# Corner copies ahead of the gates, modulation blocks ahead of turned vectors and decay, in a two-layer mixer and expert kernel

## The reference

```python
mod = jax.nn.silu(c) @ ada_w + ada_b
sh1, sc1, g1, sh2, sc2, g2 = jnp.split(mod[:, None, :], 6, axis=-1)
h = (_rms(x, norm1_g) * (1.0 + sc1) + sh1).astype(dtype)
z = h @ w_in                       # 16 column groups of 512, and a few gate columns
...                                # z is cut into p['m_q'], ..., p['n_vw'], p['n_g']
y_m = mlstm_mixer(...)             # conv on q and k, gates i and f, decay matrix, sigmoid(o)
y_b = moba_mixer(...)
y_r = retention_mixer(...)
y_n = nsa_mixer(...)               # compressed, selected (slc) and window (win) branches
y = jnp.concatenate([y_m, y_b, y_r, y_n], axis=-1).astype(dtype) @ w_out
x = x + g1 * y
h2 = (_rms(x, norm2_g) * (1.0 + sc2) + sh2).astype(dtype)
return x + g2 * hier_moe(h2, ...)  # 32 experts, every token to two of one group
```

## Time and profile before

| | us |
|---|---|
| median of 3 runs | 1665.14 |
| lowest, highest | 1665.05, 1674.46 |
| the profiled execution | 1668.25 |
| its span, first to last instruction | 1666.1 |
| TensorE busy | 1393.0 (84%) |
| VectorE busy | 595.8 (36%) |
| ScalarE busy | 187.7 (11%) |

### The profile page before, as it was taken

One profiled execution on the slowest core, in us unless ns is written; L12 is line 12 of the kernel. 1 busy time (PEld: TensorE's weight loads), 2 busy tenths in 40 slices (PEclk: granted clock), 3 DMA queues, 4 the chain that ended last, 5 costly groups with the idle time before them and its releaser, 6 DMA issues.

```text
span 1666.1 us, 17839 instructions
## 1 busy us (share of the span) xinstructions
PE 1393.0 (84%) x7389; PEld 760.7 (46%) x7389; DVE 595.8 (36%) x927; ACT 187.7 (11%) x459; POOL 31.4 (2%) x35
## 2 busy tenths in 40 slices
PE   5998999979999999998876776777677667767767
PEld 4666888758556854473422322223223223223223
DVE  4556684676445457422211221121120121122113
ACT  2001221102012100121100100100100101001001
POOL 0000000000000000010000000000000000000000
PEclk9999999989999999999988887787788788787788
DMA  9996686667758677869999999999999999999997
GB/s 397 427 426 259 251 342 272 257 246 280 268 220 328 234 291 299 361 253 421 424 429 428 428 429 428 429 429 428 428 428 428 428 429 428 428 429 429 428 429 293
DMA packets 44536, 611.90 MB, mean 367 GB/s; under 512 B 4896, under 2 KB 5168, under 8 KB 6736
## 3 DMA queue, kind: packets, MB, share of 16 engines
q1 hardware_dynamic: 42848, 604.00, 87.5%
q0 software_dynamic: 1072, 6.44, 0.9%
q10 hardware_dynamic: 576, 0.89, 0.1%
HBM read 609.21 MB, written 2.10 MB: 367 GB/s over the span
## 4 chain that ended last, share of the span: by engine, by line
PE 49%; DMA 45%; DVE 5%; issue 1%; ACT 0%; SPq 0%; POOL 0%; DVEq 0%
DMA ring<-in_exp_w 31%; DMA Zpad<-in_exp_w 10%; PE W L671 8%; PE W L658 7%; PE W L650 7%; PE M L1092 5%; PE W L1000 5%; DMA ring<-in_stream 3%; PE W L624 2%; PE A L1110 2%; PE W L1044 2%; DVE tail L1441 2%; PE W L976 2%; PE M L634 2%; PE W L1057 2%; PE M L1064 1%
## 5 line engine op out<-in xcount | busy, mean ns | idle before, releaser
L1441 DVE SCALAR_TENSOR_TENSOR tail<-ring,small,tail 128x512 f32<-128x512 f32 x300 | 225.6, 752 | 10.5
L1092 PE MATMUL M<-ring,g1b 128*32 128x512 f32 x1024 | 148.3, 711 | 62.9 <-DMA ring<-in_exp_w 62.9
L1374 DVE TENSOR_TENSOR consts<-A,tail 32x512 f32<-32x512 f32 x128 | 87.9, 686 | 162.5 <-PE A L1110 159.5
L658 PE MATMUL W<-ring,buf_h 128*128 128x512 f32 x320 | 140.7, 598 | 0.0
L1952 DVE SCALAR_TENSOR_TENSOR tail<-tail,M 128x128 f32<-128x128 f32 x32 | 9.2, 288 | 295.6 <-ACT tail L1351 295.6
L1110 PE MATMUL A<-Zpad,tail 128*32 128x512 f32 x512 | 84.5, 793 | 36.3 <-DMA Zpad<-in_exp_w 31.9
L650 PE MATMUL W<-buf_h,ring 128*128 128x256 f32 x512 | 112.0, 379 | 0.2 <-DMA ring<-in_stream 0.2
L1064 PEld LDWEIGHTS M<-consts,tail 128*128 128x128 f32 x512 | 68.4, 208 | 92.1 <-ACT tail L1353 60.0
L650 PEld LDWEIGHTS W<-buf_h,ring 128*128 128x128 f32 x512 | 96.7, 190 | 13.3 <-issue 0.4
L1092 PEld LDWEIGHTS M<-ring,g1b 128*32 128x32 f32 x1024 | 30.8, 119 | 146.5 <-DMA ring<-in_exp_w 90.4
L1092 PE MATMUL M<-Zpad,g1b 128*32 128x512 f32 x512 | 74.9, 713 | 27.0 <-DMA Zpad<-in_exp_w 27.0
(11 more groups left out here) (311 smaller groups left out, 1301.0 us busy)
## 6 DMA issues: line engine op xcount, KB each, us to landing
ring<-in_stream SPq DMA_DIRECT2D x88, 2048.0 KB, 10.3
ring<-in_exp_w SPq DMA_DIRECT2D x88, 2048.0 KB, 38.3
Zpad<-in_exp_w SPq DMA_DIRECT2D x64, 2048.0 KB, 32.1
PPY<-in_exp_w SPq DMA_DIRECT2D x24, 2048.0 KB, 30.8
tail<-in_exp_w SPq DMA_DIRECT2D x16, 2048.0 KB, 45.2
Zpad<-in_early SPq DMA_DIRECT2D x8, 1536.0 KB, 10.6
buf_x<-in_x SPq DMA_DIRECT2D x2, 1024.0 KB, 7.0
buf_h<-in_x POOLq DMA_DIRECT2D x1, 2048.0 KB, 12.3
```

The costliest lines, as they stand in the source:

```text
L658: ins = pe.matmul(dst[:, tt * 512:tt * 512 + 512], hT[:, kk, tt * P:tt * P + P], w[:, 512 * k:512 * k + 512], start=(kk == 0), stop=(kk == ...
L1092: ins = pe.matmul(M[32 * j:32 * j + 32, 512 * w13:512 * w13 + 512], XT[:, kk, 32 * q:32 * q + 32], w[:, 512 * k:512 * k + 512], start=(kk ...
L1374: return dve.tensor_tensor(o, x, y, op)
L1441: ins = dve.scalar_tensor_tensor(acc, w, cs[:, kk:kk + 1], acc, ALU.mult, ALU.add)
```

## The change

Three places of the order of steps change, and no operation is added or taken away.

1. For n_ks, ScalarE copies corners 0, 1 and 2 in the step `sums_24`, which stands ahead of `gates`; before it was corner 0 alone. Corners 3 and 4 stay in the step `chunk`. For m_o nothing changes (0 and 1 in `sums_24`), for the others neither.
2. `ada_turn` 0 is written into the list, behind `ada` 13 in place of ahead of it, and `pv slc` stands ahead of `sums_31 m_o` in place of behind it. TensorE's order is the same before and after. VectorE's is: block 13, turned vectors of block 0 (that is of blocks 8 to 11), `pv slc`, `sums_31 m_o`, `sums_24 m_o`, where it was turned vectors, block 13, `sums_31 m_o`, `pv slc`, `sums_24 m_o`.
3. `ada` 15 stands ahead of `m_decay` and `corners b_v` in place of behind them. TensorE's and the stream's order stay the same; VectorE's changes.

```diff
 EARLY = ('n_kc', 'n_vc', 'n_q')
+EARLY_CORNERS = {'n_ks': 3, 'm_o': 2}
 SEVEN = ('n_ks', 'n_vs', 'n_kw', 'n_vw', 'm_o', 'b_v')
@@
-         ('chunk', 'm_v'), ('ada', 13), ('sums_31', 'm_o'), ('pv', 'slc'), ('sums_24', 'm_o'), ('scores', 'win'),
+         ('chunk', 'm_v'), ('ada', 13), ('ada_turn', 0), ('pv', 'slc'), ('sums_31', 'm_o'), ('sums_24', 'm_o'), ('scores', 'win'),
          ('chunk', 'm_o'), ('ada', 14), ('sums_31', 'b_v'), ('turn_p', 'win'), ('sums_24', 'b_v'), ('pv', 'win'),
-         ('chunk', 'b_v'), ('m_decay', 0), ('corners', 'b_v'), ('ada', 15), ('turn_y', 'n'),
+         ('chunk', 'b_v'), ('ada', 15), ('m_decay', 0), ('corners', 'b_v'), ('turn_y', 'n'),
@@ def place_sums(order):
         elif step == 'chunk':
             placed += waiting
-            waiting = [('ada_turn', b) for s, b in waiting if s == 'ada_rows']
+            waiting = [('ada_turn', b) for s, b in waiting if s == 'ada_rows' and ('ada_turn', b) not in order]
@@ the scalar engine's program
                     copy_corner(arg, 0)
-                    if arg == 'm_o':
-                        copy_corner(arg, 1)
-                    elif arg == 'b_v':
+                    for i in range(1, EARLY_CORNERS.get(arg, 1)):
+                        copy_corner(arg, i)
+                    if arg == 'b_v':
                         act.wait_ge(sem["chunk_copied"], chunk_no('m_o'))
                         act.activation(zslot['m_o'], zslot['m_o'], ACT.Tanh, scale=0.5).then_inc(sem["gate_tanh_m"], 1)
                 elif step == 'chunk' and arg in SEVEN:
-                    for i in range(2 if arg == 'm_o' else 1, 5):
+                    for i in range(EARLY_CORNERS.get(arg, 1), 5):
                         copy_corner(arg, i)
```

## The result

| | before | after |
|---|---|---|
| median, us | 1669.4 (6 runs) | 1653.6 (6 runs) |
| lowest to highest, us | 1665.05 to 1674.46 | 1649.88 to 1657.09 |
| ratio, 95% interval | | 0.9904 [0.9876, 0.9932] |
| the profiled execution: total, span | 1668.25, 1666.1 | 1657.09, 1654.9 |

The changed kernel is 0.96% faster by the ratio; the medians of six runs each differ by 15.8 us. Two more sets of runs gave 0.9899 [0.9874, 0.9923] and 0.9894 [0.9866, 0.9922]. All three intervals hold 0.99, so whether the gain is under or over 1% isn't decided. The forecast was 15.5 us; its absolute time, 1649.6 us, rested on a median of three runs of before (1665.14), which with more runs came out 4 us higher. After's 1653.6 lies in the stated range.

The account below looks back on a forecast made before the run. TensorE was taken to bound the stage before the expert stream, DMA the stream itself. Corners 7.5, block 13 8.0 and block 15 0 sum to 15.5 us: 1665.14 to 1649.6 us, range 1644.5 to 1657.5.

Parts of the forecast that it names:

- stated range: Range given for the changed kernel's time: 1644.5 to 1657.5 us, with 5% and 14% beyond its ends.
- the rival with full clock: Clock stays full after the new stall before m_o's second half: 9.7 for 8.0 us, total 1647.9 us; chance 27%.
- What bounds: TensorE bounds about 130 to 760 us, DMA's expert stream 830 to 1600; a microsecond saved moves the stream's start by one.
- The corners: n_ks: earlier corner copies remove TensorE's 5.15 us wait and 2.4 us of clock loss, 7.5 us; bounds 5.15 to 7.5.
- Block 13: Before m_o: block 13 in VectorE's idle time removes a 9.6 us wait; gain 9.7, less 1.7 for clock, 8.0 us.
- The third coupling: m_o's corner 2, behind ScalarE's exponentials, is there at 373.2; TensorE wants it at 373.4, so it fits by 0.2 us.
- The term of 1.7 us: Behind the new 2.5 us stall before m_o's second half: one 3.5 us stretch at half clock, 1.7 us lost.
- Block 15: Moved ahead of the decay into VectorE's 16.56 us of idle time; counted as 0 us.
- Both covers: Block 15: 4.2 us of idle time left, then 12.5 us until TensorE turns yb; 16.7 us of delay in all.
- Only one wait goes: Only the n_ks or only the m_o edit bears: 7.5 or 8.0 us remain, 1657.6 or 1657.1 us; chance 14%.
- hidden: TensorE runs earlier into a transfer that doesn't move, so no gain: 1665 us; chance 9%.
- Slower: Block 15's second half lands late and holds up the decay; a 50 us delay gives about 1683 us; chance 5%.

Follow-up runs that it names:

- e7_ramp: Changed kernel with eight more 128x512 products on TensorE ahead of the expert stage's first gather; median 1657.9 us, ratio to before 0.9933.
- e2_middle: Kernel before with the middle edit alone (block 13 ahead of the turned vectors, read of slc ahead of sums_31 of m_o); 1660.7 us, ratio 0.9954.
- e0: The changed kernel itself, run once more with nothing altered; median 1652.8 us, ratio to before 0.9899.
- e6: Changed kernel with 32 more row operations of VectorE behind block 15, each waiting for the one before; 1665.9 us in one timed run.
- e8: The changed kernel again, run beside a later variant on the same chip; median 1653.0 us, ratio to before 0.9894.
- e1: Kernel before with the corner edit alone (three corner copies of n_ks ahead of the gates); median 1660.4 us, ratio 0.9956.
- v1: Changed kernel with block 0's turned vectors and the add into yb put behind the window branch's scores; measured twice, 1648.4 and 1650.7 us.

## Why the prediction was right, point by point

**The total.** The gain was forecast as 15.5 us and came out as 15.8 by the first medians, and that it is so near is in part luck. Over all timed runs the means are 17.0 us apart (standard error 0.9), which lies nearer to the 17.2 us of the rival with full clock. The mechanism, two waits of TensorE that go and a short one that comes, is shown by the traces of the parts.

**What bounds.** Right: two waits of TensorE carried the gain of the mixer stage, and a microsecond there moved the first expert issue by one (17.5 us, of which about 2 are the clock at the decay). That it moves the end as well holds on average (to within some 3 us), not in one execution: I took the expert stream as bound by DMA from its first issue on, since the share of 1.01 was read from 830 us on the earlier trace rows. In its first 60 us TensorE sets the pace, and e7_ramp shows it. That step was too coarse; it made the spread of the totals look like noise of the measurement, where part of it is the clock.

**The corners.** The sum was 7.5 us; the trace shows the third product at 151.16 for 151.1, Tanh at 151.64 for 151.6, corner 3 at 156.4 for 156.3, 8.0 us between matched executions (7.7 at m_o's second half, a little over the "7.5 at most"), and 0.44% (7.3 us) in timed runs.

**Block 13.** Durations taken from the rows gave the new wait as 2.5 us and it is 2.32; the start of the second half as 363.0 and it is 362.83 with this edit alone. The third coupling, corner 2 behind the exponentials with 0.2 us to spare, held: in e2_middle the copy ends at 373.00 and TensorE's product starts at 373.29, without a wait.

**The clock behind the new wait.** The term of 1.7 us was right as a size (8.86 us with the clock fallen, 7.17 us without it, 1.7 us) and wrong as a certainty: in the six profiles that have this wait (after, e0, e2, e6, e7, e8) the clock fell behind it in two. So the forecast and its rival of the full clock are both right in part of the executions, and the price on average is nearer to 0.6 (a third of 1.7) than to 1.7 us, as far as six executions tell. The gain of the middle edit alone, 0.46% or 7.7 us by the ratio (9.2 us by the means), doesn't tell the two apart. The section of the Trainium skill that the prediction names (TensorE: Matmul & The Clock Gate, Why this matters for your kernels) warns of long idle gaps between bursts of matmuls. Here the clock fell behind a gap of 2.32 us in two of six executions, and the measurement decides.

**Block 15.** Zero, as said: 0.9998. Both covers were measured, 4.4 us of idle time left and 16.5 us until TensorE waits.

**The rivals.** "Only one wait goes" and "hidden" fell with e1 and e2. "Slower" is real as a mechanism, by e6_cover. The chance of 31% for faster by over 1%, against 66% within, put the case near its edge, and rightly: the ratios of the three sets, 0.9904, 0.9899 and 0.9894, lie on both sides of it. That the first fell within 1% is luck.

## What to carry to other kernels

Where an engine runs dry ahead of a wait, look which of its later steps has its data already and put it in the gap; then add up what it still owes the bound engine before the next handing over, for that sum, not the order within it, sets the new wait. What nobody asks for yet (here an add and a turned vector) goes behind that handing over. And read where a stage bound by DMA really begins: the mean share of the whole stage hides an entry in which TensorE sets the pace.

## What the hardware showed

- The clock fell behind thin work without idle time too: behind 2.2 us of four-row transposes and products it was 0.51 for 3.5 us in the earlier trace rows, and the 32 matmuls that follow took 15.68 us in place of 14.00. That was so in three of 14 profiles (before and both of v1), and costs 1.7 us of a 1650 us kernel.
- The same instructions of the expert stage's first 60 us ran at a mean granted clock of 0.89 to 1.00 from one execution to the next, which goes with 971 to 972 or 975 to 976 us up to the last products. The eight last products took 11.3 or 13.1 to 13.6 us. Together it is up to 6.7 us, a good part of the scatter of 7 to 11 us between executions of one kernel.
